# Gate and up projections as seven half-size products (Strassen's form) in a hybrid decoder layer, and an out-projection by quarters of the tokens

## What is computed

```
xn  = rms_norm(x, norm_mix_g)
q, k, v, hc, gb, gc = split(xn @ w_in)            # 8 heads x 64, and 512 conv channels
attn = three dilated causal windows, merged by their softmax denominators
conv = gb * conv3(gc * hc)
h   = x + concat(attn, conv) @ w_out              # the out-projection
hn  = rms_norm(h, norm_ffn_g)
y   = h + (silu(hn @ w_gate) * (hn @ w_up)) @ w_down
y   = rms_norm(y, norm_final_g)
```

## Time and profile before

| | us |
|---|---|
| median of 3 runs (1320.06 to 1320.13) | 1320.11 |
| the profiled execution, first to last instruction (span) | 1318.2 |
| PE busy, 8,296 matmuls | 1300.3 |
| PE weight loads busy | 1212.5 |
| DVE busy | 471.1 |
| POOL busy | 498.9 |
| ACT busy | 238.4 |

### The profile page before, as it was taken

The page is one execution under the profiler, slowest core; times in us unless marked ns, Lnnn a source line. Parts: engine busy times, 40 slices in busy tenths (PEclk is TensorE's granted clock), DMA queues, the critical chain, the costliest instruction groups (busy, mean ns, idle before and its releaser), DMA issues.

```text
span 1318.2 us, 20412 instructions
## 1 busy us (share of the span) xinstructions
PE 1300.3 (99%) x8296; PEld 1212.5 (92%) x8296; DVE 471.1 (36%) x886; ACT 238.4 (18%) x506; POOL 498.9 (38%) x473
## 2 busy tenths in 40 slices
PE   7999999999999999999999999999999999999997
PEld 6997687989666799999999999999999999999997
DVE  7844222434666332940403131212212131303046
ACT  6000110000777411331000000001010101010113
POOL 3453032222654232424343433434343433344435
PEclk9999999999999999999999999999999999999999
DMA  5545466252121220101010111111111111110103
GB/s 197 204 147 204 149 220 232 69 203 80 49 86 44 84 97 33 65 16 65 32 65 33 51 46 49 48 49 48 49 49 36 45 49 48 49 49 32 65 0 134
DMA packets 38083, 107.82 MB, mean 82 GB/s; under 512 B 4016, under 2 KB 16496, under 8 KB 36208
## 3 DMA queue, kind: packets, MB, share of 16 engines
q1 hardware_dynamic: 38000, 106.60, 22.8%
HBM read 95.73 MB, written 10.85 MB: 81 GB/s over the span
## 4 chain that ended last, share of the span: by engine, by line
PE 95%; DVE 1%; ACT 1%; DMA 1%; issue 1%; POOL 1%; SPq 0%; DVEq 0%; POOLq 0%
PE ps L528 21%; PE ps L529 20%; PE ps L530 20%; PE ps L917 6%; PE ps L919 6%; PE ps L918 6%; PE ps L670 3%; PE ps L715 2%; PE ps L694 2%; PE ps L647 1%; PE ps L649 1%; PE ps L648 1%; PE ps L621 1%; PE ps L593 1%; DMA resid<-in_xT 1%
## 5 line engine op out<-in xcount | busy, mean ns | idle before, releaser
L528 PE MATMUL ps<-act_hi,w_hi 128*128 128x352 f32 x1608 | 522.5, 325 | 9.0 <-DVE act_lo L1236 9.0
L529 PE MATMUL ps<-act_lo,w_hi 128*128 128x352 f32 x1608 | 516.0, 321 | 0.0
L530 PE MATMUL ps<-act_hi,w_lo 128*128 128x352 f32 x1608 | 515.8, 321 | 0.0
L528 PEld LDWEIGHTS ps<-act_hi,w_hi 128*128 128x128 f32 x1608 | 302.2, 188 | 23.2 <-issue 22.7
L529 PEld LDWEIGHTS ps<-act_lo,w_hi 128*128 128x128 f32 x1608 | 302.8, 188 | 0.3
L530 PEld LDWEIGHTS ps<-act_hi,w_lo 128*128 128x128 f32 x1608 | 301.8, 188 | 0.0
L397 POOL TENSOR_TENSOR gate_cell<-ones 128x1 f32<-128x1 f32 x90 | 18.3, 203 | 667.8 <-PE ps L530 445.3
L401 POOL TENSOR_TENSOR w_lo<-w_stage,w_hi 128x1024 fp32r<-128x1024 f32 x91 | 220.3, 2421 | 7.3
L1569 DVE TENSOR_TENSOR work<-ps,work 128x352 f32<-128x352 f32 x66 | 34.4, 524 | 442.2 <-PE ps L530 442.2
L917 PE MATMUL ps<-pair_hi,w_hi 128*128 128x352 f32 x504 | 162.7, 323 | 0.0
L1579 DVE TENSOR_TENSOR resid<-ps,resid 128x352 f32<-128x352 f32 x240 | 125.9, 525 | 102.8 <-PE ps L919 102.8
(11 more groups left out here) (237 smaller groups left out, 1230.0 us busy)
## 6 DMA issues: line engine op xcount, KB each, us to landing
w_stage<-in_w SPq DMA_DIRECT2D x97, 512.0 KB, 3.5
resid<-in_state_k SPq DMA_DIRECT2D x8, 1792.0 KB, 7.5
v_buf<-in_state_v SPq DMA_DIRECT2D x14, 1024.0 KB, 5.1
resid<-in_xT SPq DMA_DIRECT2D x16, 528.0 KB, 7.5
out_yT<-resid SPq DMA_DIRECT2D x24, 176.0 KB, 2.1
q_d<-out SPq DMA_DIRECT2D x12, 176.0 KB, 4.3
out_kT<-out SPq DMA_DIRECT2D x12, 176.0 KB, 2.0
out_v<-out SPq DMA_DIRECT2D x16, 128.0 KB, 1.8
```

Of the source, the lines that this page charges most:

```text
L528: pe.matmul(out, hi, rhs_hi, start=first, stop=False)
L529: pe.matmul(out, hi, rhs_lo, start=False, stop=False)
L530: return pe.matmul(out, lo, rhs_hi, start=False, stop=last)
```

## The change

The products of the feed-forward's first half are written as a 2 x 2 block product. For a block f of 128 hidden channels the stationary side holds gate and up weights, each with two halves of the input channels; the moving side is hn, cut into two halves of the input channels and two of the tokens (528 each): A11, A12 (first tokens), A21 and A22. Strassen's form in Winograd's variant computes gate and up of both token halves with seven products in place of eight:

- seven moving operands of 4 x 528 elements a row: A11, A12, A22 and the sums S1, S2, S3, S4 (`MOVING`), made once by DVE (`normal`, `combined`), with high parts by ACT (`combo_high`) and low parts by POOL (`combo_low` of POOL) or, for S2 and S4, by DVE.
- for each f four sums of weights of 128 x 512 (`weight_sums`, `last_weight_sum`) by DVE in the raw weights, split by POOL in half units (`gate_split`).
- seven products a block, P1, P2, P6, P7, P5, P4, P3 (`PRODUCTS`), each 4 x 2 x 3 = 24 matmuls of 264 columns into two banks (`gate_job`). P6 and P5 are added into P1's banks and P3 too, P4 into P7's; between them ACT copies the banks out (`keep_p1`, `keep_u2`, `keep_p7`) and DVE adds up (`first_gate`, `second_up`, `second_gate`).
- blocks 0 and 1 are interleaved in an order of their own (`FIRST_GATES`). Then for each pair: the even block's products, the down jobs of the pair before, the odd block's products; in the last pair the down jobs follow the odd block.
- odd blocks and the down jobs share banks 6 and 7, so the odd block's P1 waits for all down adds (`added`); even blocks use banks 2 and 3.
- the out-projection runs by quarters of the tokens (264 columns, 32 jobs), with sums over halves: `sum_of_squares(0)` behind job 25, `sum_of_squares(1)` behind the first product.
- DVE, ACT, POOL and SP are written out without loops; SP has three weight buffers for two, and the convolution's tail is stored before x is loaded again.

The core of the diff:

```diff
-            for j in range(2, NC * KT):
+            for j in range(2, OUT_JOBS):
                 out_job(j)
-                if j in SUMS_BEHIND:
-                    sum_of_squares(SUMS_BEHIND.index(j))
...
+                if j == SUM_BEHIND:
+                    sum_of_squares(0)
+            def gate_job(f, product):
+
+                pos = POS[f, product]
+                bank = {"P2": 4, "P4": 0, "P7": 0}.get(product, 6 if f % 2 else 2)
+                pe.wait_ge(half_split, SPLIT_NO[pos])
+                if product == "P1":
+                    if f == 0:
+                        pe.wait_ge(h_done, OUT_JOBS - 3)
+                    elif f == 1:
+                        pe.wait_ge(mean_sq, NC + 2)
+                    elif f % 2 and f < FT - 1:
+                        pe.wait_ge(added, 12 * (f - 1))
+                    else:
+                        pe.wait_ge(hidden1, f - 1)
+                elif product == "P2":
+                    if f:
+                        pe.wait_ge(gate1, f)
+                    else:
+                        pe.wait_ge(h_done, OUT_JOBS)
+                        pe.wait_ge(h_ss, OUT_JOBS)
+                elif product == "P7" and f:
+                    pe.wait_ge(gate2, f)
+                elif product == "P6":
+                    pe.wait_ge(p1_kept, f + 1)
+                elif product == "P5":
+                    pe.wait_ge(u2_kept, f + 1)
+                elif product == "P3":
+                    pe.wait_ge(up2, f + 1)
+                elif product == "P4":
+                    pe.wait_ge(p7_kept, f + 1)
+                hi, lo = w_hi_row[:, slots(pos)], w_lo_row[:, slots(pos)]
+                x_hi, x_lo = MOVING[product]
+                first = product in ("P1", "P2", "P7")
+                for x in range(2):
+                    out, tk = ps[:, bank + x, 0:QC], slice(QC * x, QC * x + QC)
+                    for k in range(4):
+                        if f == 0 and x == 0:
+                            done, n = FIRST_LOWS[product]
+                            pe.wait_ge((pool_lo, dve_lo)[done], n + k + 1)
+                        wk = slice(P * k, P * k + P)
+                        pe.matmul(out, hi[:, wk], x_hi[:, k, tk], start=(k == 0 and first), stop=False, skip_group_check=not first)
+                        pe.matmul(out, hi[:, wk], x_lo[:, k, tk], start=False, stop=False, skip_group_check=not first)
+                        mm = pe.matmul(out, lo[:, wk], x_hi[:, k, tk], start=False, stop=(k == 3), skip_group_check=not first)
+                mm.then_inc(gate_done, 1)
...
+            def weight_sums(f):
+
+                g, u = raws[LOAD["gate", f] % RAWS], raws[LOAD["up", f] % RAWS]
+                if f:
+                    dve.wait_ge(half_split, max(SPLIT_NO[POS[f - 1, "P5"]], SPLIT_NO[POS[f - 1, "P6"]]))
+                dve.wait_ge(raw_in[LOAD["gate", f] % RAWS], 16 * (LOAD["gate", f] // RAWS + 1))
+                dve.wait_ge(raw_in[LOAD["up", f] % RAWS], 16 * (LOAD["up", f] // RAWS + 1))
+                dve.tensor_tensor(t1, u[:, 0:512], g[:, 0:512], ALU.subtract).then_inc(t_made, 1)
+                dve.wait_ge(t_made, 4 * f + 1)
+                dve.tensor_tensor(t2, u[:, 512:1024], t1, ALU.subtract).then_inc(t_made, 1)
+                dve.tensor_tensor(u[:, 0:512], u[:, 512:1024], u[:, 0:512], ALU.subtract).then_inc(t_made, 1)
+
+            def last_weight_sum(f):
+
+                g = raws[LOAD["gate", f] % RAWS]
+                dve.wait_ge(half_split, SPLIT_NO[POS[f, "P2"]])
+                dve.wait_ge(t_made, 4 * f + 3)
+                dve.tensor_tensor(g[:, 512:1024], g[:, 512:1024], t2, ALU.subtract).then_inc(t_made, 1)
+
+            def first_gate(f):
+
+                dve.wait_ge(gate_done, GATE_NO[f, "P2"])
+                dve.wait_ge(p1_kept, f + 1)
+                dve.tensor_tensor(b1[f % 2], two_banks(4), b1[f % 2], ALU.add).then_inc(gate1, 1)
...
+            normal(y21, 0, 0, 1)
+            normal(y21, 1, 1, 1)
+            combined(s3_f, y11, y21, 0, ALU.subtract, Y21_AT[0])
+            normal(y21, 2, 2, 1)
+            combined(s3_f, y11, y21, 1, ALU.subtract, Y21_AT[1])
+            normal(y21, 3, 3, 1)
+            combined(s3_f, y11, y21, 2, ALU.subtract, Y21_AT[2])
+            first_gate(0)
+            combined(s3_f, y11, y21, 3, ALU.subtract, Y21_AT[3])
+            for k in range(4):
+                normal(y22, k, k + 4, 1)
+            last_weight_sum(0)
...
+            for f in range(2, FT):
+                p = f // 2 - 1
+                first_gate(f)
+                second_up(f)
+                if f % 2 and f < FT - 1 or f == FT - 2:
+                    weight_sums(f + 1)
+                second_gate(f)
+                second_hidden(f)
+                hidden_low2(f)
+                first_hidden(f)
+                if f % 2 == 0 and f < FT - 2:
+                    add_down(p, 0)
+                    add_down(p, 1)
+                    hidden_low1(f)
+                    add_down(p, 2)
+                    weight_sums(f + 1)
+                    for i in range(3, NC * KT):
+                        add_down(p, i)
+                        if i == 12:
+                            last_weight_sum(f + 1)
+                else:
+                    hidden_low1(f)
+                    if f < FT - 1:
+                        last_weight_sum(f + 1)
...
+PRODUCTS = ["P1", "P2", "P6", "P7", "P5", "P4", "P3"]
+FIRST_GATES = [(0, "P1"), (0, "P2"), (1, "P1"), (1, "P2"), (0, "P7"), (0, "P4"), (0, "P6"), (0, "P5"),
+               (1, "P6"), (0, "P3"), (1, "P7"), (1, "P5"), (1, "P4"), (1, "P3")]
+def feed_forward():
+
+    order = list(FIRST_GATES)
+    loads = [(what, f) for f in range(2) for what in ("gate", "up")]
+    for p in range(1, PAIRS):
+        even, odd = ([(f, n) for n in PRODUCTS] for f in (2 * p, 2 * p + 1))
+        gates = [[("gate", f), ("up", f)] for f in (2 * p, 2 * p + 1)]
+        down, downs = [("down", p - 1)], [("down", 2 * p - 2), ("down", 2 * p - 1)]
+        last = p == PAIRS - 1
+        order += even + (odd + down if last else down + odd)
+        loads += gates[0] + (gates[1] + downs if last else downs + gates[1])
+    order.append(("down", PAIRS - 1))
+    return order, loads + [("down", FT - 2), ("down", FT - 1)]
```

735 lines of the change are left out of this document (453 added, 282 removed).

## The result

The changed kernel takes **1350.6 us** (median of 4 runs, 1350.2 to 1352.1), against 1320.1 before, run beside it: a ratio of 1.0234, 95% interval 1.0219 to 1.0248. It is slower by 30.5 us, where 1309 was predicted, with a range that ended at 1329. The profiled execution spans 1348.4 us.

A forecast was written before the change was run, and what follows sets the result against it. PE, busy for 99%, was taken to bound the kernel. From span 1318.2, -62.1 + 0.2 + 25.8 + 22.8 + 2.0 = -11.3 gave 1306.9, and 1.9 for the median 1309 us; range 1290 to 1329.

The forecast's parts named there:

- five waits at the start: First 14 feed-forward products: PE waits for squares 3.5, first gate 6.2, A22 5.3, S2 3.8, t2 5.4 us.
- three in a pair: Down jobs and odd block's P1: waits of 1.35 behind weight sums, 0.8 at P1, 0.3 behind last_weight_sum, 2.4 us together.
- Step 4 (pairs): Pairs of blocks: waits cost 21.6 us in nine pairs and 1.2 more at down(9), 22.8 us in all.
- step 3: Feed-forward start: DVE's SBUF sums and POOL's work hardly overlap; PE's waits, with 1.6 us from the out-projection, total 25.8 us.
- the 7 us of work in 20: Inside the products: DVE needs only about 7 of 20.1 us a block, so it has room.
- Steps 1 and 2 (the pace): Products and out-projection: matmuls of 264 columns take 119.4 ns, saving 62.1 us in products and adding 0.2 in the out-projection.
- third rival: Products no faster per column: 264 columns cost over 122 ns, gain gone at 121.9, 1334 us at 125; chance 0.13.
- step 1: Feed-forward products: weight loads run under matmuls, so 3,696 matmuls take 441.3 us instead of 503.4, saving 62.1.
- Step 5 (the clock): Waits at the feed-forward start: one fall of PE's clock to 1.2 GHz, booked at 2 us.
- Costly columns: Matmuls of 264 columns in products and out-projection are slowed by weight loads: above 1322 us; chance 0.13.
- Strict turns: DVE and POOL alternate: the start costs 38 us, the pairs lose 8 more, 1317 to 1330 us; chance 0.17.
- The waits are small: Start costs 16 us, pairs 13, no clock fall: 1287 at the least, 1294 with half of each; chance 0.22.

The follow-up runs named there:

- experiment 1: Changed kernel with down results in four banks in turn instead of two: 1317.6 us, ratio to the kernel before 0.9978.
- experiment 2: Changed kernel with hidden_low2 of even blocks moved behind down add 9: 1337.6 us, ratio to the kernel before 1.0134.
- experiment 3: Changed kernel with POOL's subtraction for feed-forward weight low parts cut to 16 columns, the rest left out: 1328.7 us, one run.
- experiment 4: Kernel before, with nine series of 48 matmuls of 128 to 512 columns added at its end: 264 columns took 121.7 ns a matmul.
- experiment 7: Changed kernel, unaltered, profiled a second time: 1354.4 us, one run, start 78.2 us for 75.4.
- experiment 5, busy: Changed kernel with 50 dummy matmuls of 264 columns ahead of PE's wait for the first gate: 1353.7 us, one run.
- experiment 5: Three single edits on the changed kernel: first gate add earlier, 1352.6 us; block 1's weight sums earlier, 1352.8; dummy matmuls on PE, 1353.7.
- experiment 8: S3, A22, S1 low parts moved from POOL to DVE, last_weight_sum(0) earlier, on four banks plus moved hidden_low2: 1301.6 us for 1307.0; with three start edits too, 1303.7.
- the three edits of the start: First gate earlier, block 1's weight sums earlier, sum of squares behind job 26; added to four banks and moved hidden_low2: 1309.7 us, against 1307.0 without.

## Why the prediction was wrong

It had the right terms, and its five waits at the start and three in a pair came where it put them. What it lacked was one more wait in the pairs, and the size of two terms. Waits in this part are PE's time beyond the pace.

- **Step 4 (pairs), +24.8 of the 41.5 us between the predicted and the measured span.** It failed at "first_hidden, two adds, hidden_low1 and add 2 end at 3.7 us behind the first down job's start": that takes it that DVE is free when the job ends. In the pair shown above add 2 ended 5.8 us behind that start, since second_hidden and hidden_low2 stand ahead and POOL's split holds them for a microsecond each. This is the wait of 2.0 us by the third down job in seven of nine pairs; experiments 1, 2 and 3 show it from three sides. By the pairs of experiment 2, 66.8 us for 68.5 on average, it cost 16.0 us. The other three waits came to 2.9 us a pair where 2.4 was booked, 4.2 in all: behind the weight sums (1.35 predicted, 1.2 to 1.3 measured), at P1 (0.8; 0.9), behind last_weight_sum (0.3; 0.4), and 0.1 more behind each of the first and last, where the next matmul too came late. In the last down jobs 1.2 was booked; 3.3 came at down(9), with 1.6 behind it at the lower clock, and 0.9 ahead of the last group's jobs. I had the very rule for it in step 3, and used it at the start only; the 7 us of work in 20 said nothing, as two banks give PE a slack of less than one job.
- **Steps 1 and 2 (the pace), +8.9.** 264 columns take 121.4 ns, not 119.4. The third rival's first point, "over 122", was nearly met: a gain was left, 12% less than booked. Proportion to columns, right from 352 to 512, does not hold near the 112 ns that the series of 128 to 220 columns all took; experiment 4 measures it with nothing else running. By the Trainium skill (TensorE: Matmul & The Clock Gate, Back-to-back issue gap), about 81 ns go to a load and a matmul of 128 columns; here the series of 128 took 112.3 each, and the measurement decides. That loads run under matmuls, as step 1 read from the earlier trace rows, held: each of these matmuls has a load of its own, recorded with 0.19 us, and starts 0.121 behind the one before.
- **Step 3 (the start), the waits, +1.0.** Squares 3.7 us (3.5 predicted), first gate 6.9 (6.2), A22 2.4, 1.2, 1.0 and 1.0 in four pieces (5.3), S2 0.5, 1.2 and 1.3 (3.8), t2 3.2 (5.4): all within 2.3 us, and in sum what step 3 gave. One more, of 1.05 us, was not in its list ("P7, P5, P3 wait for nothing more"): P5 of block 0 stands right behind P6, whose result ACT has to copy out first (`keep_u2`). The price of holding was right for this execution, one operation of DVE for each of POOL's; the second execution of the same program went otherwise (experiment 7).
- **Step 5 (the clock), +6.6.** I booked one fall, 2 us, "as PE is not the last one there". The lower level lasted for 89 matmul distances, at 0.220 for 0.121: 8.6 us. Yet holding the clock up behind the longest wait won nothing that one run could show (experiment 5, busy). If the start is bound by DVE and POOL, as experiments 5 and 8 suggest, this term and the waits are one sum, and the reason was right where the number was not.
- **Rivals.** Costly columns came near but did not decide. None of them had the mechanism that did: a slow DVE ahead of the down adds. "Strict turns" gave it 0.3 us a place, far too little. In "The waits are small" the sum is off too: with half of each of its three terms (5, 5 and 1 us) it gives 1298, not 1294.

For a kernel without that wait the number would have held, and by luck: 1307.0 was measured with four banks and the low part moved, by wrongs that nearly cancel (the pace and the start cost some 17 us more than booked, the pairs and the last down jobs 20 less).

**Open.** Why the cast is held in some executions and not in others; what the three edits of the start do one by one with the pairs mended; what the moved weight sum gave in experiment 8; and whether DVE could be let through by another order on POOL, which was not tried.

## What to carry to other kernels

When a producer job gets shorter or an engine behind it gets more work, write down for every bank ring how late the freeing instruction may be, and walk its queue from what stands ahead of it, with the durations that those instructions have beside the other engine's work; a ring of two gave less than one job of slack, and here two more banks were worth 33 us. A saving in matmul columns is to be priced at a measured pace of that width, not in proportion. Work with two SBUF inputs may be better put on the faster of DVE and POOL, even on the busier one, where either holds the other: it was in the one place where this was tried, with 5.4 to 6.0 us.
